# Pooling inside the attentions, router bias by one product, values ahead of the last turns, one weight slab in a place of its own

## The reference

```
px = modulate(rms_norm(x)) @ w_in          # q, k, v of A and B, pooled input u, gates
y_a = GQA with rotary (8 query heads, 2 key heads); y_b = neighbourhood attention (4 heads)
y_c = pool_mixer(u): d = windowed mean(u) - u ; y = (d per group @ pool_w) * pool_scale
m = sigmoid(g_a)*(y_a @ w_pa) + sigmoid(g_b)*(y_b @ w_pb) + sigmoid(g_c)*(y_c @ w_pc)
x = x + g1 * (m @ w_out)
# layer 1's second half:
logits = h @ router_w + router_b           # h = rms_norm(x)*scale + shift
```

## Time and profile before

| | us |
|---|---|
| median of 3 runs | 1946.44 (1946.33 to 1947.47) |
| the profiled execution, whole | 1946.46 |
| its span in the trace | 1944.6 |
| PE busy | 1900.7 (98%) |
| DVE busy | 603.1 (31%) |
| ACT busy | 449.6 (23%) |
| POOL busy | 409.3 (21%) |
| mean granted clock of PE | 0.994 |

### The profile page before, as it was taken

The page is one execution under the profiler, slowest core; times in us unless marked ns, Lnnn a source line. Parts: engine busy times, 40 slices in busy tenths (PEclk is TensorE's granted clock), DMA queues, the critical chain, the costliest instruction groups (busy, mean ns, idle before and its releaser), DMA issues.

```text
span 1944.6 us, 48442 instructions
## 1 busy us (share of the span) xinstructions
PE 1900.7 (98%) x22336; PEld 1386.6 (71%) x22337; DVE 603.1 (31%) x1194; ACT 449.6 (23%) x759; POOL 409.3 (21%) x126
## 2 busy tenths in 40 slices
PE   6999999999999999999999999999999999999997
PEld 4875888898888888968986666666666666666664
DVE  4355332253632545475541011110211111120112
ACT  4357322243222224465440000100000000000001
POOL 2400444435546454304530000000000000000000
PEclk8999999999999999999999999999999999999999
DMA  8352332226353655303589999999999999999990
GB/s 343 133 197 85 111 101 95 89 86 238 132 193 133 238 224 185 130 23 131 174 311 384 403 408 382 377 381 408 398 375 397 387 408 380 380 393 401 409 375 25
DMA packets 70144, 506.60 MB, mean 261 GB/s; under 512 B 7793, under 2 KB 8049, under 8 KB 9265
## 3 DMA queue, kind: packets, MB, share of 16 engines
q1 hardware_dynamic: 69552, 501.08, 66.3%
q0 software_dynamic: 384, 2.36, 0.3%
HBM read 502.36 MB, written 1.05 MB: 259 GB/s over the span
## 4 chain that ended last, share of the span: by engine, by line
PE 82%; issue 9%; POOL 5%; DMA 1%; DVE 1%; ACT 1%; SPq 0%; DVEq 0%; POOLq 0%; ACTq 0%
PE bank L1525 30%; PE bank L1537 14%; PE bank L937 10%; PE bank L939 10%; PE bank L938 10%; POOL w_lo L583 5%; DMA start_slab<-in_w_mod 1%; PE pv_bank L1288 1%; PE turned_pair L1270 1%; PE bank L972 1%; PE bank L1246 0%; PE bank L1539 0%; PE bank L1251 0%; PE turned_pair L1511 0%; PE bank L1511 0%
## 5 line engine op out<-in xcount | busy, mean ns | idle before, releaser
L1525 PE MATMUL bank<-moe_slab,HE 128*32 128x256 f32 x10752 | 592.8, 379 | 1.3 <-DVE GT L2847 1.3
L1525 PEld LDWEIGHTS bank<-moe_slab,HE 128*32 128x32 f32 x10752 | 348.7, 110 | 231.2 <-DVE GT L2847 1.8
L583 POOL TENSOR_TENSOR w_lo<-slab,w_hi 128x2048 fp32r<-128x2048 f32 (+3 forms) x88 | 369.0, 4196 | 540.3 <-ACT w_hi L1742 540.3
L937 PE MATMUL bank<-H_HI,w_hi 128*128 128x512 f32 (+1 forms) x912 | 321.6, 353 | 0.4 <-POOL H_LO L851 0.3
L938 PE MATMUL bank<-H_LO,w_hi 128*128 128x512 f32 (+1 forms) x912 | 319.6, 350 | 0.0
L939 PE MATMUL bank<-H_HI,w_lo 128*128 128x512 f32 (+1 forms) x912 | 319.5, 350 | 0.0
L1537 PE MATMUL bank<-moe_slab,GE 128*32 128x256 f32 x4032 | 299.8, 379 | 0.0
L1539 PE MATMUL bank<-moe_slab,GE 128*32 128x256 f32 x1344 | 299.1, 379 | 0.0
L1537 PEld LDWEIGHTS bank<-moe_slab,GE 128*32 128x32 f32 x4032 | 166.6, 110 | 115.0
L2844 DVE TENSOR_TENSOR GT<-SE,bank 128x256 f32<-128x256 f32 x56 | 23.6, 421 | 631.8 <-ACT SE L2082 631.8
L2080 ACT ACTIVATE SE<-bank 128x256 f32<-128x256 f32 x56 | 21.4, 383 | 772.0 <-PE bank L1525 772.0
(11 more groups left out here) (289 smaller groups left out, 2022.9 us busy)
## 6 DMA issues: line engine op xcount, KB each, us to landing
moe_slab<-in_moe_up SPq DMA_DIRECT2D x224, 1024.0 KB, 7.3
moe_slab<-in_moe_w SPq DMA_DIRECT2D x112, 1024.0 KB, 7.2
slab<-in_w_in SPq DMA_DIRECT2D x38, 1024.0 KB, 4.9
slab<-in_ffn_w SPq DMA_DIRECT2D x30, 1024.0 KB, 4.9
row_slab<-in_w_mod_rows SPq DMA_DIRECT2D x28, 1024.0 KB, 7.1
start_slab<-in_w_mod SPq DMA_DIRECT2D x8, 1024.0 KB, 17.1
slab<-in_w_proj SPq DMA_DIRECT2D x8, 1024.0 KB, 4.8
slab<-in_w_out SPq DMA_DIRECT2D x8, 1024.0 KB, 4.9
```

The costliest lines, as they stand in the source:

```text
L583: engine.tensor_tensor(lo, raw, hi.bitcast(F32), ALU.subtract).then_inc(done, 1)
L937: mm(out, lhs[0], rhs[0], start=start, stop=False)
L1525: ins = mm(outs[t // 2][32 * b:32 * b + 32, 256 * (t % 2):256 * (t % 2) + 256], rows[t], w[:, 256 * b:256 * b + 256], start=first and t != ...
```

## The change

1. Layer 0: each of the two fills of pool products stands in one of the last two steps on PE (n = 16 and 17), ahead of the turning; ACT copies each to the pooled tile behind its `turned_copy` of that step. The products with the pooling weights stand behind the last value products, and ACT stores them after its last `result`.
2. Layer 1: both fills of pool products stand ahead of step 0, the pooling weights in step 1 behind `scores(3)`; ACT copies the first in step 0 and stores the second in step 1. The pooled tile is DT, now at 90 KB, in layer 0, and an unused half of QK in layer 1.
3. The router bias: DVE multiplies `router_w` by the shifts (64 columns), PE sums over the partitions with one product by ones in step 2, and DVE reduces over the chunks and adds `router_b` after its division of step 3.
4. In the last two steps of both layers the value products stand ahead of the turning of their step instead of behind it.
5. Slab 2 of layer 0 has place 2 for its own, and POOL makes its low part ahead of the three transfers. The slabs behind it change places (0 for 1) and wait for another slab's last product.

```diff
@@ -224,15 +224,21 @@
         if layer == 0:
             mod(mod_beside(layer, 0))
         else:
-            fills.append(("router_bias",))
+            fills.extend(("pool", 1, p) for p in range(2))
         for n in range(steps):
             scores(n + 2)
+            if layer == 1 and n == 1:
+                fills.extend(("poolw", 1, p) for p in range(2))
+            if layer == 1 and n == 2:
+                fills.append(("router_bias",))
+            if layer == 0 and n >= steps - 2:
+                fills.append(("pool", 0, n - steps + 2))
             if n and mod_beside(layer, n) is not None:
                 mod(mod_beside(layer, n))
             if turned_beside(layer, n) is not None:
                 turned_mod(turned_beside(layer, n))
-        fills.extend(("pool", layer, p) for p in range(2))
-        fills.extend(("poolw", layer, p) for p in range(2))
+        if layer == 0:
+            fills.extend(("poolw", 0, p) for p in range(2))
         for j in range(4):
             slabs.extend(("in", layer, W_IN_GATE + 4 * b + j) for b in range(3))
             fills.extend(("gate", layer, j, b, m) for b in range(3) for m in range(2))
@@ -273,7 +279,7 @@
 
 
 
-OWN_PLACE = {("w1", 0, 0): 2, ("in", 1, W_IN_BK): 3, ("w3", 0, 0): 4, ("in", 1, W_IN_KV): 4}
+OWN_PLACE = {("in", 0, W_IN_KV): 2, ("w1", 0, 0): 2, ("in", 1, W_IN_BK): 3, ("w3", 0, 0): 4, ("in", 1, W_IN_KV): 4}
 IN_TURN = [k for k in SPLITS if k not in OWN_PLACE]
 SPLIT_PLACE = {**{k: n % 2 for n, k in enumerate(IN_TURN)}, **OWN_PLACE}
 
@@ -400,7 +406,7 @@
                        for k in ((0, 1), (0, 2), (1, 1), (1, 2))}
                       for n, kb, kb_ in (("SQ_SUM", 176, 96), ("SQ", 180, 98)))
         TMP = at("TMP", 184, [P, 2, T])
-        DT = at("DT", 164, [P, 2, T])
+        DT = at("DT", 90, [P, 2, T])
         H_FIRST = at("H_FIRST", 168, [P, 4, T])
         H_NEW = at("H_NEW", 88, [P, 4, T])
         PW = at("PW", 188, [P, 2, P])
@@ -608,6 +614,10 @@
 
             return slice(S * s, S * s + S)
 
+        def pooled(layer, p):
+
+            return DT[:, p, :] if layer == 0 else QK[:, p, S:T]
+
         def x_range(layer):
 
             return (0, T) if layer == 0 else (S, T)
@@ -861,9 +871,10 @@
             next_low_part()
             h_low_parts(LOW_BY_POOL[2:])
 
+            next_low_part()
             pool.dma_start(POOL[:].rearrange("p a g n -> p (a g n)"), a["pool_mat"]).then_inc(pool_in[0], 16)
             small_loads(0)
-            for _ in range(2, W_IN_GATE + 2):
+            for _ in range(3, W_IN_GATE + 2):
                 next_low_part()
 
             wait_full(pool, ("poolw", 0, 1))
@@ -1294,39 +1305,52 @@
                 if layer == 0:
                     mod(mod_beside(layer, 0))
                 else:
-                    router_bias()
+                    for p in range(2):
+                        pool(1, p)
                 for n in range(len(steps)):
                     if n + 2 < len(steps):
                         scores(n + 2)
+                    if layer == 1 and n == 1:
+                        pool_weights(1)
+                    if layer == 1 and n == 2:
+                        router_bias()
+                    late = n >= len(steps) - 2
+                    if layer == 0 and late:
+                        pool(0, n - len(steps) + 2)
                     if n and mod_beside(layer, n) is not None:
                         mod(mod_beside(layer, n))
                     if turned_beside(layer, n) is not None:
                         turned_mod(turned_beside(layer, n))
+                    ended = last_step(layer, n - 1) if n else None
+                    if late and ended is not None:
+                        values(ended, n - 1)
                     turn(n)
-                    if n and last_step(layer, n - 1) is not None:
-                        values(last_step(layer, n - 1), n - 1)
+                    if not late and ended is not None:
+                        values(ended, n - 1)
                 values(len(pairs) - 1, len(steps) - 1)
-
-            def pooling(layer):
+                if layer == 0:
+                    pool_weights(0)
+
+            def pool(layer, p):
                 pe.wait_ge(pool_in[layer], 16)
 
                 for m in (range(2) if layer == 0 else (1,)):
                     wait_taken(pe, ("in", layer, ("u", m)))
-                for p in range(2):
-                    out = fill(("pool", layer, p))
-                    for n, stream in enumerate(streams_of(layer)):
-                        for gg in range(2):
-                            g = 2 * p + gg
-                            ins = chain(out[HD * gg:HD * gg + HD, S * n:S * n + S],
-                                        [(U[:, 2 * stream + t, HD * g:HD * g + HD], POOL[:, t, g, :])
-                                         for t in range(2)])
-                    filled(ins, ("pool", layer, p))
+                out = fill(("pool", layer, p))
+                for n, stream in enumerate(streams_of(layer)):
+                    for gg in range(2):
+                        g = 2 * p + gg
+                        ins = chain(out[HD * gg:HD * gg + HD, S * n:S * n + S],
+                                    [(U[:, 2 * stream + t, HD * g:HD * g + HD], POOL[:, t, g, :]) for t in range(2)])
+                filled(ins, ("pool", layer, p))
+
+            def pool_weights(layer):
                 nq = S * len(streams_of(layer))
                 pe.wait_ge(pw_in, 16 * (layer + 1))
                 for p in range(2):
                     out = fill(("poolw", layer, p))
                     wait_taken(pe, ("pool", layer, p))
-                    filled(mm(out[:, 0:nq], PW[:, p, :], DT[:, p, 0:nq], start=True, stop=True), ("poolw", layer, p))
+                    filled(mm(out[:, 0:nq], PW[:, p, :], pooled(layer, p), start=True, stop=True), ("poolw", layer, p))
 
             BRANCH_CHUNKS = (range(0, 4), range(4, 6), range(6, 8))
 
@@ -1445,12 +1469,9 @@
             def router_bias():
 
                 out = fill(("router_bias",))
-                pe.wait_ge(row_parts_made, 3)
-                for k in range(DC):
-                    lo = VEC_COLS["rw"][0] + N_EXPERTS * k
-                    ins = mm(out[:, 0:N_EXPERTS], mod_vec(1, 3, k, LAT).to_broadcast([P, P]), VEC[:, lo:lo + N_EXPERTS],
-                             start=k == 0, stop=k == DC - 1)
-                filled(ins, ("router_bias",))
+                pe.wait_ge(router_ready, 2)
+                filled(mm(out[:, 0:DC * N_EXPERTS], ones, small["t1"][:, 0:DC * N_EXPERTS], start=True, stop=True),
+                       ("router_bias",))
 
             def route():
                 logits = fill(("logit",))
@@ -1677,7 +1698,6 @@
                 else:
                     first_in_proj()
                 attention(layer)
-                pooling(layer)
                 merge(layer)
                 out_proj(layer)
                 if layer == 0:
@@ -1975,7 +1995,14 @@
                         exps(n + 1)
                     if ended(n - 2) is not None:
                         result(ended(n - 2))
+                    if layer == 1 and n == 0:
+                        for p in range(2):
+                            pool_out(1, p)
                     turned_copy(n)
+                    if layer == 1 and n == 1:
+                        pool_weights_out(1)
+                    if layer == 0 and n >= len(steps) - 2:
+                        pool_out(0, n - len(steps) + 2)
                 if ended(len(steps) - 2) is not None:
                     result(ended(len(steps) - 2))
 
@@ -1985,13 +2012,17 @@
                 for _ in range(2):
                     high_part()
                 result(len(pairs) - 1)
-
-            def pooling(layer):
+                if layer == 0:
+                    pool_weights_out(0)
+
+            def pool_out(layer, p):
                 nq = S * len(streams_of(layer))
-                for p in range(2):
-                    key = ("pool", layer, p)
-                    wait_full(act, key)
-                    af(DT[:, p, 0:nq], acc(key)[:, 0:nq], ACT.Copy).then_inc(freed(key), 1)
+                key = ("pool", layer, p)
+                wait_full(act, key)
+                af(pooled(layer, p), acc(key)[:, 0:nq], ACT.Copy).then_inc(freed(key), 1)
+
+            def pool_weights_out(layer):
+                nq = S * len(streams_of(layer))
                 for p in range(2):
                     key = ("poolw", layer, p)
                     wait_full(act, key)
@@ -2291,12 +2321,18 @@
                                 g.unsqueeze(2).to_broadcast([P, DC, 4, N_EXPERTS]),
                                 scales.unsqueeze(3).to_broadcast([P, DC, 4, N_EXPERTS]), ALU.mult)\
                     .then_inc(router_ready, 1)
+                shifts = MOD[1][:, 6 * DC:8 * DC].rearrange("p (k s) -> p k s", s=2)[:, :, 0:1]
+                v.tensor_tensor(small["t1"][:, 0:DC * N_EXPERTS].rearrange("p (k e) -> p k e", k=DC), g,
```

(11 more changed lines are left out.)

## The result

After took 1953.68 us (median of 12 runs, 1949.77 to 1955.42), before, run beside it, 1946.27 (1944.04 to 1948.35): ratio 1.0036 [1.0027, 1.0044], by the ratio some 7.0 us slower (5.3 to 8.6), by the two medians 7.4. The profiled execution took 1954.78, span 1953.0 (before 1946.46 and 1944.6).

A forecast was written before the change was run, and what follows sets the result against it. PE, 82% of the chain, was taken as the bound. Order terms of -1.3 + 3.1 + 2.1 - 2.4 = +1.5 us plus +2.8 for the clock made +4.3 on 1946.46: 1950.8 us, range 1945.5 to 1953.2.

The forecast's parts named there:

- slab 2: Slab 2 in layer 0: its high part no longer waits 3.40 us for PE; gain 1.3 us.
- layer 0's end, order: Layer 0's last two attention steps: turn 17 behind pool fill and value products makes high part and gate 3.1 us later.
- layer 1, first steps, order: Start of layer 1's attention: bank rotation makes scores(4) wait for step 3's exponentials, turn 2 2.1 us later.
- layer 1, last steps: End of layer 1's attention: value products fill the wait ahead of turn 10, copies end 2.4 us sooner.
- low clock after the new waits: Three new long PE waits, ahead of both layers' gates and scores(4): two followed by low clock, +2.8 us.
- the price of the row: Upper bound per low stretch, 1.68 us: the profiled 16 value products taking 3.63 instead of 1.95 us at turn 10.
- rival of three falls: Clock falls behind all three new PE waits at 1.68 us each: +6.5 us, 1953.0; chance 0.18.

The follow-up runs named there:

- e1: The kernel before with only slab 2's own place and its POOL low part ahead of the transfers: 1944.67 us, ratio 0.9991.
- e2: The kernel before with only layer 0's end changed: pool fills ahead of turns 16 and 17, value products ahead of turn 17: 1950.83 us, ratio 1.0025.
- e4b: The kernel before with only layer 0's value products ahead of its last turning, pooling left at the end: 1948.14 us, ratio 1.0006.
- e3: The kernel before with only layer 1's pooling and router bias moved inside the attention: 1951.39 us, ratio 1.0037, five executions.
- e6: The kernel after with layer 0's end as before and layer 1's pooling weights again behind its last value products: 1943.17 us, ratio 0.9985.
- e4: The kernel before with only layer 1's value products ahead of its last turnings: 1945.21 us, ratio 0.9993.
- e5: The kernel after with filler products, results unused, in PE's three long waits: 1949.25 us, ratio 1.0015.
- m1: The kernel before with slab 2's own place and low-part order plus layer 1's value products ahead of its last turnings: 1943.21 us, ratio 0.9987.
- m2: The e6 kernel with two filler products, results unused, in PE's wait ahead of layer 1's gates: 1944.02 us, ratio 0.9985.

## Why the prediction was wrong

By its own steps, in us:

| step | forecast | rows of the pair | what the runs say |
|---|---|---|---|
| slab 2 | -1.3 | -1.5 | e1: -1.8 (-3.5 to 0) |
| layer 0's end, order | +3.1 | +2.9 | e2; e4b: 0.7 of it is value products |
| layer 1, first steps, order | +2.1 | +2.6 | e3, e6: 3.96 against a before without its fall |
| layer 1, last steps | -2.4 | -2.65 | e4: -1.4 (-3.1 to +0.4) |
| low clock after the new waits | +2.8 | +5.8 | e5: 1.66 + 1.6, and 2.5 by its pace |
| sum | +4.3 | +7.2 | +7.0 (5.3 to 8.6) |

The pair's spans differ by 8.4: 7.2, the late start of 1.38, and -0.2 left over. With 2.4 for the last fall, as from the gates to the end of the span, the sum is 7.0 and nothing is left.

**The failed step** is the clock: "Each low stretch costs at most 1.68, the price of the row; I take 1.4", and "With two of the three waits followed by a low stretch, + 2.8". It failed in both factors. All three waits were followed by a fall, and the one ahead of layer 1's gates cost 2.5, above my upper bound. The bound came from the earlier trace rows and a low stretch of 3.4 us (879.2 to 882.6) that PE filled without a gap. The stretch at the gates lasted 6.8 us (894.8 to 901.7), 5.8 of them behind the wait. It is this length that cost more, and not the products: in e6 the same gates ran as closely through a low stretch of 3.4 us, which at their pace (3.3 us x 0.44) cost 1.5. What makes the stretch twice as long is not shown: it was so behind the waits of 3.32 us in after and e3 (891.0 to 897.8), not behind those of 3.30 ahead of layer 0's gates. The rival of three falls had the right mechanism, 0.18 and 1953.0; its price was low too. The range had the same bound in it, and so ended too early.

**What was right.** Each order came as written: the pool fill, the value products and then turn 17; ACT in line for it (3.10 us); `scores(4)` behind ACT's exponentials (2.32 us, forecast 2.45); both gates waiting for POOL (3.30 and 3.32 for 3.5 and 3.4); value products in the wait ahead of turn 10. Their sum was +1.5 and measured +1.4.

**What was right by luck.** In two terms the order and before's own falls were mixed. The first steps went from 10.12 us (m1, clock 1.00) to 14.08 (e3, clock 1.00): 3.96. Before's 11.42 holds 1.30 of a fall that I had not looked for, behind the 16 small products and a wait of 0.58; the new order doesn't have it, so only 2.66 showed. Of the 3.96, the pool fills ahead of `scores(2)` and the new bias product make 0.76 (e6: 10.88), the two fills of the pooling weights with ACT's stores of them the other 3.2. The last steps' -2.65 are 1.68 of a fall not had and 0.97 of order; with the 1.30 they make the 3.94 us by which m1 is shorter from first scores to gates. Without any clock the parts come to -1.5 + 2.9 + 3.96 - 0.97 = +4.4: the order was the larger half of the loss, and the falls that before paid, 1.30 + 1.68, hid part of it.

The Trainium skill (TensorE: Matmul & The Clock Gate, section "HAM oscillation — how this bites in real kernels") says that waits between bursts throttle the array again, at a loss of half the throttled time. The page's example has waits for DMA that are longer than the 2.32 us ahead of `scores(4)`, so that all three places fall does not follow from it alone, as the prediction had it; but they did; half of the time is also what the paces here give (0.44 to 0.47). I had weighed it against one row and counted two of three. e3's wait of 2.32 us at clock 1.00 shows that it isn't so each time.

What stays open: why one wait is followed by a fall in one execution and not in another. After's twelve times lie in two groups, three at 1949.8 to 1950.4 and nine at 1952.7 to 1955.4; a fall more or less would fit, but only one of them was traced, and their mean granted clocks do not sort them (0.994 for the three, 0.992 to 0.996 for the nine). A forecast of 1950.8 is near the group of three, the median lies in the other.

## What to carry to other kernels

Work of the bottleneck engine that stands behind its last hand-over covers the next stage's preparation; moved ahead of that hand-over it delays the preparation and leaves a bare wait. Before a wait is priced from one row, all low-clock stretches of the trace have to be listed, the old kernel's too: a fall costs nearly half of the low stretch for which products run back to back, and the stretch itself came in two lengths here. Fills put between others shift which bank waits for which: here two of them cost 3.2 us where their work on PE is 1.2.

## What the runs showed of the hardware

The same waits recur in the eleven profiled executions wherever a kernel has their place, so their falls can be counted; why one falls and another doesn't is open. A wait of 3.3 us ahead of gates was followed by a low clock in 4 of 4 (after twice, e2, e3); one of 2.25 to 2.32 in 2 of 3 (after and e6, not e3); the one of 2.08 ahead of turn 10 in 4 of 5 (before, e1, e2, e4b, not e3); one of 1.9 to 2.0 for POOL near 990 us in 3 of 11 (e5, e6, m2). The 16 products of 8 columns with a wait of 0.58 behind them were followed by one in 5 of 6 (not in m1); the five kernels with the pool products in their place had none there (after, e3, e5, e6, m2). A low stretch in the middle of the run lasted 3.4 us, at layer 1's gates in after and e3 6.8. The price was 1.3 us for one of 3.4 with turnings and scores in it (before, m1), 1.5 to 1.7 where PE filled it without a gap (before, after, e6), and 2.4 to 2.5 for the one of 6.8 in after, of which 1.0 lay in the wait.
